# Latent attention with two heads side by side, its fillers on two banks, the last gates made after the last exponentials, and the output's second pass begun inside it

## The reference

```
q = concatenate([q[..., :128], apply_rope(q[..., 128:], cos, sin)])   # k likewise
def one_block(args):                                 # per 128 queries, 4 heads
    s = jnp.einsum('bhqd,bhkd->bhqk', q_blk, kt) * scale
    s = jnp.where(key_idx[None, :] <= q_idx[:, None], s, -jnp.inf)
    p = jax.nn.softmax(s, axis=-1)
    return jnp.einsum('bhqk,bhkd->bhqd', p, vt)
o_mla = block_causal_attention(q, k, v) * jax.nn.silu(m_gate)
x = x + jnp.concatenate([o_gla, o_mla], axis=-1) @ w_out[l]
```

## Time and profile before

| | |
|---|---|
| time, median of 3 runs | 1873.46 us (1870.86 to 1874.4) |
| profiled execution: its time, its span | 1872.61 us, 1870.8 us |
| PE busy | 1814.6 us, 97% |
| DVE busy, ACT busy | 1030.0 us (55%), 824.0 us (44%) |
| attention and output product, layer 0 | 1531.60 to about 1618.1 us in the span |
| the same, layer 1 | 1781.03 to about 1867.5 us in the span |

### The profile page before, as it was taken

How to read it: one execution, slowest core, us unless ns; L and a number is a source line. 1 busy time by engine, 2 the same in 40 slices (tenths; PEclk the granted TensorE clock), 3 DMA queues, 4 the chain that set the end, 5 groups by cost and what they waited for, 6 DMA issues and landing times.

```text
span 1870.8 us, 23280 instructions
## 1 busy us (share of the span) xinstructions
PE 1814.6 (97%) x9667; PEld 1467.5 (78%) x9667; DVE 1030.0 (55%) x1595; ACT 824.0 (44%) x1295; POOL 23.9 (1%) x21
## 2 busy tenths in 40 slices
PE   8997899999999999999999999999999999999998
PEld 6886888888888887777788888888877866778666
DVE  5676665454533545776675444433467555556553
ACT  5657653333332344565464333332364353443442
POOL 0000100000000000000100000000000000000000
PEclk9998999999999999999999999999999999999999
DMA  5331222223233222111222322333222121222111
GB/s 201 102 102 46 79 81 100 90 93 109 91 101 100 80 91 68 46 46 47 78 81 89 105 98 90 99 105 95 85 82 84 57 68 34 79 90 80 46 45 45
DMA packets 44200, 154.83 MB, mean 83 GB/s; under 512 B 5024, under 2 KB 5184, under 8 KB 44096
## 3 DMA queue, kind: packets, MB, share of 16 engines
q1 hardware_dynamic: 44096, 153.36, 25.1%
HBM read 150.19 MB, written 2.10 MB: 81 GB/s over the span
## 4 chain that ended last, share of the span: by engine, by line
PE 81%; issue 6%; DVE 6%; ACT 5%; DMA 0%; POOLq 0%; SPq 0%; POOL 0%; DVEq 0%; ACTq 0%
PE bank L449 81%; DVE tmp L1707 1%; DVE wl L1716 1%; ACT wh L1115 1%; ACT XH L1115 1%; ACT tmp L1115 1%; ACT X L1115 1%; PE bank L1078 0%; DVE acc_q L1704 0%; DVE XL L1716 0%; ACT Y L1115 0%; ACT L1118 0%; DVE gates L1707 0%; DVE X L1704 0%; DMA wraw<-in_wstream 0%
## 5 line engine op out<-in xcount | busy, mean ns | idle before, releaser
L449 PE MATMUL bank<-XH,wh 128*128 128x512 f32 (+1 forms) x1712 | 650.6, 380 | 35.5 <-DVE XL L1716 16.8
L449 PE MATMUL bank<-XL,wh 128*128 128x512 f32 (+1 forms) x1712 | 633.8, 370 | 0.0
L449 PE MATMUL bank<-XH,wl 128*128 128x512 f32 (+1 forms) x1712 | 633.5, 370 | 0.0
L1716 DVE TENSOR_TENSOR wl<-wraw,wh 128x1024 fp32r<-128x1024 f32 x278 | 339.2, 1229 | 295.5 <-ACT wh L1115 295.5
L1115 ACT ACTIVATE wh<-wraw 128x1024 fp32r<-128x1024 f32 x278 | 291.6, 1055 | 280.8 <-PE bank L449 274.1
L449 PEld LDWEIGHTS bank<-XH,wh 128*128 128x128 f32 x1712 | 326.0, 190 | 104.6 <-issue 26.7
L449 PEld LDWEIGHTS bank<-XH,wl 128*128 128x128 f32 x1712 | 326.4, 191 | 54.8
L449 PEld LDWEIGHTS bank<-XL,wh 128*128 128x128 f32 x1712 | 326.5, 191 | 52.9 <-issue 2.6
L449 PE MATMUL bank<-HH,wh 128*128 128x512 f32 (+1 forms) x428 | 160.4, 375 | 4.7 <-ACT PP L1115 4.7
L1704 DVE SCALAR_TENSOR_TENSOR tmp<-bank,prm,tmp 128x511 f32<-128x511 f32 x88 | 66.0, 750 | 172.0 <-ACT tmp L1115 170.4
L449 PE MATMUL bank<-HL,wh 128*128 128x512 f32 (+1 forms) x428 | 158.1, 369 | 0.0
(11 more groups left out here) (285 smaller groups left out, 2115.1 us busy)
## 6 DMA issues: line engine op xcount, KB each, us to landing
wraw<-in_wstream SPq DMA_DIRECT2D x278, 512.0 KB, 3.5
X<-in_xt SPq DMA_DIRECT2D x8, 256.0 KB, 6.0
out<-X SPq DMA_DIRECT2D x8, 256.0 KB, 2.0
pts<-in_pt SPq DMA_DIRECT2D x4, 256.0 KB, 3.9
cst<-in_consts SPq DMA_DIRECT2D x1, 810.0 KB, 8.8
kpa<-lr SPq DMA_DIRECT2D x4, 128.0 KB, 3.8
kpb<-lr SPq DMA_DIRECT2D x8, 64.0 KB, 2.9
acc_s<-in_pos SPq DMA_DIRECT2D x1, 256.0 KB, 4.0
```

What stands on the lines that cost most here:

```text
L449: return pe.e.matmul(o, l, r, start=start, stop=stop, skip_group_check=True)
L1716: return dve.e.tensor_tensor(o, x, h.bitcast(F32), ALU.subtract)
```

## The change

Heads are worked in twos (0 with 1, then 2 with 3). `QB` and `HEAD` give block and head of the 16 results. PE does both heads' parts without position, then both rotary parts, then both masks; each step n then has two transposes with a filler portion before and between them. Scores use banks 0 to 3, transposes 4 and 5, fillers and head outputs 6 and 7. The second head of a two gets a place of its own for its transposed result (`PTs[1]`, in `gates` 0 to 3, free by then), a fourth `tmp`, and `sqr` for the gated output. `table(SILU)` and `silu(3)` move behind the last exponentials, and `table(LNEXP)` goes. The output's k = 4 and 5 blocks for columns 0 to 3 are done between the last transposes and the last two head outputs, then k = 6 and k = 7 for these columns, then columns 4 to 7 as before. The weight stream is reordered to match.

```
-        o += [(f"out{layer}", k, c) for c in range(8) for k in range(4, KD)]
+        o += [(f"out{layer}", k, c) for c in range(4) for k in (4, 5)] + [(f"out{layer}", k, c) for k in (6, 7) for c in range(4)]
+        o += [(f"out{layer}", k, c) for c in range(4, 8) for k in range(4, KD)]
...
+    m.PTs = [m.PT, m.gates[:, 0:4, :]]
...
+HEAD = [j // 8 * 2 + j % 2 for j in range(16)]
+QB = [j // 2 % 4 for j in range(16)]
+A_SCORES, A_TURN, A_OUT, A_SIDE = [0, 1, 2, 3], [4, 5], [7, 7, 7, 6], [6, 7, 6, 7, 6, 6, 7, 6]
+OUT_BANK = [2, 3, 0, 1, 2, 3, 4, 5]
...
 (TensorE)
+                if c < 2:
+                    pe.wait_ge(s.gv, 8 * layer + 7 + c)
+                elif c == 6:
+                    pe.wait_ge(s.at_u, 4 * layer + 2)
                 else:
+                    pe.wait_ge(s.out_a, 8 * layer + (0, 0, 1, 2, 3, 5, 0, 6)[c])
...
-            mm(o[:, 0:n], m.qraw[h][:, qs], m.kraw[h][:, 0:n], True, False)
-            mm(o[:, 0:n], m.qr[r, h // 2, qs], m.krh[r, h // 2, 0:n], False, False)
-            mm(o[:, qs], m.identb[:, :], m.mml[:, :], False, True).then_inc(s.at_s, 1)
+            for hh in range(2):
+                mm(o[hh][:, 0:w_], m.qraw[2 * i + hh][:, qs], m.kraw[2 * i + hh][:, 0:w_], True, False)
+            for hh in range(2):
+                r = slice(64 * hh, 64 * hh + 64)
+                mm(o[hh][:, 0:w_], m.qr[r, i, qs], m.krh[r, i, 0:w_], False, False)
+            for hh in range(2):
+                mm(o[hh][:, qs], m.identb[:, :], m.mml[:, :], False, True).then_inc(s.at_s, 1)
...
+        for n in range(9):
+            if n < 8:
+                att_scores(n)
+            if n == 5:
+                att_out(0)
             next(side, None)
+            if n == 5:
+                att_out(1)
+            if n:
+                att_turn(2 * n - 2)
+                next(side, None)
+                att_turn(2 * n - 1)
+        out_rest([0, 1], (4, 5))
+        att_out(2)
+        out_rest([2], (4, 5))
+        att_out(3)
+        out_rest([3], (4, 5))
+        out_rest(range(4), [6])
+        out_rest(range(4), [7])
+        for c in range(4, 8):
+            out_rest([c], range(4, KD))
...
 (ScalarE)
-        table(SILU)
         feed_group("ukv" + L, range(1), range(4, 8))
-        silu(3)
...
-        table(LNEXP)
...
+        for n in range(9):
+            if n < 8:
+                att_scores(2 * n)
+                att_scores(2 * n + 1)
+            else:
+                table(SILU)
+                silu(3)
...
 (VectorE, behind the loop)
+        feed_group("out" + L, (4, 5), range(4))
+        att_out(2)
+        att_out(3)
+        att_low(2)
+        feed_group("out" + L, [6], range(4))
+        att_low(3)
+        feed_group("out" + L, [7], range(4))
```

More of the change, by code:

```diff
@@ L1050, in tensor_program, with att_scores @@
         side = halves()
[L1051 to L1055, removed]
+        def att_scores(n):
+            i, qb = n // 4, n % 4
+            w_, qs = 128 * (qb + 1), slice(qb * 128, qb * 128 + 128)
+            o = [bank[A_SCORES[(2 * n + hh) % 4]] for hh in range(2)]
+            if n >= 2:
+                pe.wait_ge(s.at_p, 16 * layer + 2 * n - 2)
             else:
@@ L1075, in att_turn @@
+        def att_turn(j):
+            o = bank[A_TURN[j % 2]]
+            if j >= 2:
+                pe.wait_ge(s.at_t, 16 * layer + j - 1)
+            else:
+                pe.wait_ge(s.gv, 8 * layer + 8)
             pe.wait_ge(s.at_n, 16 * layer + j + 1)
[L1076 removed]
+            for kb in range(QB[j] + 1):
                 c = slice(kb * 128, (kb + 1) * 128)
[L1078 removed]
+                ins = pe.e.transpose(o[:, c], m.tmp[j % 4][:, c], C("ident"))
@@ L1099, in tensor_program, with out_rest @@
[L1099 to L1108, removed]
+        def out_rest(cs, ks):
+            for c in cs:
+                if c < 4:
+                    pe.wait_ge(s.at_p, 16 * layer + 16)
+                elif c < 6:
+                    pe.wait_ge(s.xsum, 40 + 8 * layer + c - 3)
+                else:
+                    pe.wait_ge(s.at_t, 16 * layer + 16)
+                for k in ks:
+                    pe.wait_ge(s.mt, 8 * layer + k + 1)
+                    block("out" + L, k, c, bank[OUT_BANK[c]][:, :], XH[:, k, :], XL[:, k, :], k == 4, k == KD - 1)
@@ L1662, in att_scores @@
         def att_scores(j):
-            qb = j % 4
-            n = 128 * (qb + 1)
-            o = bank[TURNS.index(("s", j)) % 4]
+            n = 128 * (QB[j] + 1)
             act.wait_ge(s.at_m, 16 * layer + j + 1)
[L1667 to L1671, removed]
+            if j >= 4:
+                act.wait_ge(s.at_tr, 16 * layer + j - 3)
@@ L1677, in att_turn @@
             act.wait_ge(s.at_tr, 16 * layer + j + 1)
[L1678 to L1690, removed]
-            next(side, None)
+            if j >= 8:
+                act.wait_ge(s.at_o, 4 * layer + j % 2 + 1)
+            else:
+                act.wait_ge(s.mt, 8 * layer + 4)
@@ new lines, in att_out, with att_low @@
+        def att_out(h):
+            dve.wait_ge(s.at_o, 4 * layer + h + 1)
+            dve.wait_ge(s.gate, 8 * layer + 5 + h)
+            tt(sqr[h % 2][:, :], bank[A_OUT[h]][:, :], m.gates[:, 4 + h, :], ALU.mult).then_inc(s.at_u, 1)
+        def att_low(h):
+            dve.wait_ge(s.mt_h, 8 * layer + 5 + h)
+            less(XL[:, 4 + h, :], sqr[h % 2][:, :], XH[:, 4 + h, :]).then_inc(s.mt, 1)
+        for n in range(9):
+            if n < 8:
+                att_scores(n)
+            if n == 5:
+                att_out(0)
+            next(side, None)
+            if n == 5:
+                att_out(1)
+                att_low(0)
+            if n:
+                next(side, None)
+            if n == 5:
+                att_low(1)
```

112 lines of the change are left out of this document (53 added, 59 removed).

## The result

The changed kernel takes 1849.21 us (median of 4, 1848.78 to 1850.65) against 1872.91 (4, 1870.86 to 1874.4) for the kernel before. The medians differ by 23.7 us; the ratio is 0.9879, with a 95% interval of 0.9866 to 0.9891. The forecast was 1850.

A forecast was written before the change was run, and what follows sets the result against it. PE, busy 97% of the span, was taken as the bound. Terms of 5.9 + 0.7 + 2.1 + 1.6 + 1.3 = 11.6 us a layer, 23 for two, gave 1850 us (1846 to 1854; 8 in 10: 1845 to 1858).

The forecast's parts named there:

- Rotary parts and stepping: PE's scores: each pair's second rotary part costs nothing, 5.9 us a layer; fewer steps between matmul forms, 0.7 us.
- The rival that they don't overlap: PE's scores: neighbouring rotary parts don't run side by side, 11.8 us are missing, 1862 us; 6%.
- The start: Attention's start: earlier gv copies cut PE's wait at the first filler from 2.36 to 0.2 or 0.3 us; 2.1 us a layer.
- the clock: First fillers: without the long wait PE's granted clock doesn't fall (0.60 over 4.28 us); 1.6 us a layer.
- The end: Attention's end: PE's idle time before the last head outputs and output blocks is covered; 1.3 us a layer (0 to 2).
- The two new gaps: Attention's end: PE waits 0.3 us for head 2's low part and 0.2 us for column 4's bank.
- Moved at no cost: Fillers, masks, transposes, blocks and stream DMAs keep their number, the gates' Silu moves; no added time, 2 us spare on DVE.
- The slower rival: Attention steps: the softmax on DVE becomes the bound; at 1.5 us a step 1892 us; 3%.
- The small wait that I feared at n = 5: Step n = 5: head 1's output takes bank 7 from head 0's, with only 0.3 us to spare.
- the rival of 1851.5 us: ACT's table load at the end: a drain of about 1.38 us makes the last copies 0.7 us late in each layer.
- The sum: Both layers: the terms add to 11.6 us a layer, 23 us for two.
- The rival of small waits or falls: Inside the pairs: three or four waits of 0.5 us or clock falls of 1.6 us a layer give 1853 to 1858; 14%.

The follow-up runs named there:

- e1: Changed kernel with each head's scores done to the end before the other head's begin, so no two rotary matmuls are neighbours; 1862.54 us, ratio 0.9945.
- e5: Changed kernel with the first head's mask between the two rotary matmuls, parts without position still together; 1861.23 us, ratio 0.9940.
- e2: Changed kernel with both table loads and the two Silu back in front of the XH and gv copies; 1856.00 us, ratio 0.9909.
- e8: Changed kernel with three parts undone at once: heads apart, gates and table loads early, second pass late; 1870.89 us, ratio 0.9995 to the kernel before.
- e6: Changed kernel with one needless table load ahead of the XH copies; 1852.41 us, ratio 0.9895.
- e3: Changed kernel with both last head outputs done before all k = 4 and 5 blocks of columns 0 to 3; 1851.57 us, ratio 0.9886.
- e10: Changed kernel with head 2's low part ahead of head 3's output on DVE; 1848.30 us, ratio 0.9877.
- e4: Kernel before the change, with the Silu table load and two Silu moved behind the gv copies; 1869.34 us, ratio 0.9984.
- e9: Changed kernel run again with no edit; 1848.86 us, ratio 0.9877.
- e7: Changed kernel with table loads and two Silu right behind the gv copies instead of behind the last exponentials; 1849.95 us, ratio 0.9878.

## Why the prediction was right, point by point

**Rotary parts and stepping: 6.6 us forecast, 6.9 measured** (e1). 1.06 us for two `krh` of 512 columns, by the row of two neighbours, is what the timeline shows. e5 closes the question left open (what keeps them apart): neither two banks nor the accumulation does, a full-array matmul between them does. The overlap is 5.8 us (5.9 forecast). The steps between forms are 1.1 in e1, more than the 0.7 forecast, but part of that belongs to e1 alone: its second head's part without position stands right behind a mask and holds PE 1.01 us at width 512, where one of the kernel before holds it 0.95. Against the kernel before, both parts take 1.82 us (1571.52 to 1573.34) in place of 1.90, about the forecast. The rival that they don't overlap fell.

**The start, 2.1 us, and the clock, 1.6 us: 3.7 together, 4.0 measured** (e2). The wait went to nothing where I had left 0.2 to 0.3. The fall of the clock (4.28 us at 0.60) is gone, and e2 brings it back with the wait: 2.40 + 1.6. The term for the clock was the least certain. Over the twelve traces the clock fell at the first filler in all six cases with a wait of 1.8 us or more (before, e2 and e8, both layers) and in none of the other eighteen, e6's two waits of 1.36 us among them. So the fall goes with the wait, and not with the place in the program. Whether a wait of 1.36 us never brings one, two cases can't say; the last section has a place where waits of one length went both ways.

**The end: 1.3 us forecast, 1.5 and 1.2 measured** (e3). That these agree is partly luck, since e3 doesn't measure what I had counted. I took 1.9 us of idle time of the kernel before and let the early second pass cover it. Its wait of 0.8 us for a scaled `tmp` is gone in e3 and e8 too, where the second pass is late: the new order in twos, with its banks and fillers, clears it. And of the 1.3 us for `PT` that the second pass does cover in e3, about 1 us is there only because the gates' Silu now stands ahead of ACT's last copies; without it (e8) the wait is 0.2. So the second pass mainly pays for moving the gates. The last copies are in time with 1.4 us to spare, not 0.7. The two new gaps were forecast as 0.3 and 0.2 us and are 0.15 and 0.24, but the second stands in another place: I put it to column 4, which waits for a bank behind a low part and a `wl`; it is k = 7, which waits for head 3's low part behind that `wl` (e10).

**Moved at no cost.** The list of waits is empty in both layers, so the fillers, the scores in pairs and DVE's longer queue cost no more than the two small gaps. The slower rival (DVE behind in the pairs) fell with it. The caution of the Trainium skill, "TensorEngine Tiling (Array Packing)", PSUM Bottleneck, speaks of a fourfold speed-up of TensorE; here, where only the rotary parts go twice as fast, the empty list shows no such bound. The small wait that I feared at n = 5 isn't there.

**The table load.** Silu starts 1580.02 - 1578.73 = 1.29 us behind the load's start, as before the change, and in e4 an exponential stands 1.30 us behind one. So what the Trainium skill, "ScalarE: Activation LUTs", What ACT_TABLE_LOAD costs, adds for a drain (about 1.38 us) doesn't show here, and the rival of 1851.5 us fell.

**The sum.** 11.6 us a layer was forecast. Measured are 11.95 (A) and 12.17 (B), 24.1 in all. The changed kernel's profiled execution comes to the attention 0.84 us later, in earlier code that hasn't changed; so the spans differ by 23.3, and the medians by 23.7. (The forecast set the median 0.85 us above the profiled execution. With the fourth run it is 0.30, which would have made the sum 1849.7.) The three terms, undone one by one, make 12.1 of B's 12.17 us and 12.4 of A's 11.95. They aren't independent, though: e8 keeps 1.1 us of A and 1.5 of B with all three undone. That part is mostly shorter waits of PE, which my sum had under the end; which piece of the rest (order of the pairs, banks, fillers on two banks) gives them no run takes alone. The rival of small waits or falls was right in kind only: falls of the clock elsewhere move single runs by more than any new wait in the layers.

## What to carry to other kernels

Two matmuls on 64 rows each, one on the lower and one on the upper half, shared the array here as direct neighbours (1.06 us for both) and not with a full-height matmul between them (1.06 and 1.05): put such pairs side by side in PE's written order and count two as one. Work on an in-order engine that stands ahead of what PE waits for should leave that place, but count what is behind it then: e4 freed PE's start by 4 us and gave half back, because the softmax chain behind started no earlier. Undo parts of a change together as well as alone: e8 showed that one part paid for another. And where a change is worth a few us, compare like stretches of the traces beside the medians: here the stretches repeated to 0.01 us (e9), and what lies ahead of them didn't.

## What was not expected of the hardware

**Nearly the same code, different start.** Up to the attention, the changed kernel and its variants run nearly the same program, yet layer 0's first scores stand between 1530.20 (e5) and 1535.24 us (e6). The changed kernel itself repeated within 0.25 us (e9), but the 15 runs of the kernel before beside e1 to e4 spread from 1870.87 to 1874.53. The granted clock falls at a few places, not at all of them in each profile. One is the stretch from 170 to 180 us, with a mean clock of 0.66 in the kernel before and 0.53 in the changed one. Of another, these are the busy times in the changed kernel and then in e6:

```profile
1440.00:1450.00 10.00, 6.49 (x53) 4.80 (x53) 8.75 (x14) 3.15 (x5) 0.00 (x0) 1.00 0.27 86
```

```profile
1440.00:1450.00 10.00, 6.96 (x26) 5.31 (x25) 9.49 (x15) 3.40 (x4) 0.00 (x0) 0.73 0.21 58
```

Around there PE has waited for a scaled `tmp` in both, 2.77 us in the changed kernel (first row) and 2.76 in e6 (second):

```profile
1444.59 0.66 PE L893 MATMUL bank<-cst,tmp 128*128 128x128 f32 x4 [2.77 <-DVE tmp L1746]
```

```profile
1445.33 1.12 PE L893 MATMUL bank<-cst,tmp 128*128 128x128 f32 x4 [2.76 <-DVE tmp L1747]
```

The clock stays whole around the one; at the other it is at the half level from about 1444.5 us on, while PE still waits, till about 1451.3 (it falls in e1, e3, e4 and e7 too; in before, e2, e5, e8, e9 and e10 it doesn't). A wait of 1.85 us near 1369, which all twelve traces have, comes with a fall in e7 alone. At the first filler the falls came around the end of waits of 1.8, 2.2 and 2.4 us, in both layers each, and not with 1.36. So a wait's length doesn't settle by itself whether the clock falls. What else does stays open.
